# Two layers written out, and each first projection taken by halves of the rows

## The reference, cut to what matters

```python
for l in range(2):                                  # the two layers
    h = h + rmsnorm(mixer(rmsnorm(h, g1[l]) @ w_in[l], ...), g2[l])   # q, k, v of attention, then gated linear attention
    h = h + rmsnorm(swiglu(rmsnorm(h, g3[l])), g4[l])
# the block: the gain is (1 + scale), and a shift is added; both come from c @ w_ada
# then forgetting attention, block attention, and 32 experts of which each row takes 4
```

## Time and profile before

| | |
|---|---|
| median of 3 runs | 1845.13 us (1838.79 to 1845.82) |
| the profiled execution's own time | 1840.45 us |
| its span (first to last instruction) | 1838.5 us, mean granted TensorE clock 0.993 |
| TensorE busy | 1756.8 us, 96% of the span |
| its weight loads | 1038.4 us, 56% |
| VectorE, ScalarE, GpSimd busy | 638.6, 477.6, 123.4 us |

### The profile page before, as it was taken

How to read it: one execution, slowest core, us unless ns; L and a number is a source line. 1 busy time by engine, 2 the same in 40 slices (tenths; PEclk the granted TensorE clock), 3 DMA queues, 4 the chain that set the end, 5 groups by cost and what they waited for, 6 DMA issues and landing times.

```text
span 1838.5 us, 21928 instructions
## 1 busy us (share of the span) xinstructions
PE 1756.8 (96%) x8623; PEld 1038.4 (56%) x8623; DVE 638.6 (35%) x952; ACT 477.6 (26%) x632; POOL 123.4 (7%) x209
## 2 busy tenths in 40 slices
PE   7989999999999999999999999999999999899996
PEld 6776888787678888885534433333334333333332
DVE  3576666546666667242310111111011110011111
ACT  4364443234544333442211111111111111111111
POOL 1031111201111111001000000000000000000000
PEclk9999999999999999999999999999999999999999
DMA  7244776632267776563699999999998999999995
GB/s 272 78 161 150 239 257 230 247 134 96 94 193 252 243 264 225 171 237 113 283 428 428 430 402 405 429 429 428 430 398 346 430 429 430 430 428 430 430 429 248
DMA packets 116361, 559.68 MB, mean 304 GB/s; under 512 B 7460, under 2 KB 52800, under 8 KB 91576
## 3 DMA queue, kind: packets, MB, share of 16 engines
q1 hardware_dynamic: 105904, 526.47, 71.1%
q0 software_dynamic: 9728, 31.94, 5.6%
q10 hardware_dynamic: 648, 0.14, 0.0%
HBM read 557.45 MB, written 1.06 MB: 304 GB/s over the span
## 4 chain that ended last, share of the span: by engine, by line
PE 76%; DMA 12%; issue 5%; DVE 4%; ACT 2%; POOL 0%; ACTq 0%; POOLq 0%; DVEq 0%; SPq 0%
PE PA L1980 13%; DMA ring<-w_down 11%; PE PB L1980 10%; PE PA L2039 5%; PE PB L2039 5%; PE PC L1571 2%; PE PA L1797 2%; PE PD L1797 2%; PE PA L1798 2%; PE PD L1798 2%; PE PD L1804 2%; PE PA L1804 2%; PE PC L2076 2%; PE PD L2076 2%; PE PB L1571 2%
## 5 line engine op out<-in xcount | busy, mean ns | idle before, releaser
L1101 DVE TENSOR_TENSOR ring_rounded<-ring,ring_rounded 128x4096 fp32r<-128x4096 f32 (+2 forms) x53 | 213.1, 4022 | 128.8 <-ACT ring_rounded L776 128.8
L1980 PE MATMUL PA<-ring,HT 128*64 128x512 f32 x944 | 210.0, 595 | 0.2 <-issue 0.2
L1980 PE MATMUL PB<-ring,HT 128*64 128x512 f32 x864 | 194.3, 596 | 6.9 <-DMA ring<-w_gate_up 6.9
L776 ACT ACTIVATE ring_rounded<-ring 128x4096 fp32r<-128x4096 f32 (+2 forms) x53 | 174.9, 3304 | 70.5 <-PE PD L1834 32.8
L2039 PE MATMUL PA<-ring,HT 128*64 128x512 f32 x392 | 135.4, 615 | 8.7 <-DMA ring<-w_down 8.7
L1980 PEld LDWEIGHTS PA<-ring,HT 128*64 128x64 f32 x944 | 66.2, 137 | 131.2 <-issue 131.2
L1980 PEld LDWEIGHTS PB<-ring,HT 128*64 128x64 f32 x864 | 59.5, 137 | 126.5 <-issue 109.3
L2039 PE MATMUL PB<-ring,HT 128*64 128x512 f32 x392 | 127.6, 592 | 0.0
L1480 DVE TENSOR_SCALAR gla<-PA 128x512 f32<-128x512 f32 x17 | 11.8, 692 | 312.2 <-PE PA L1988 312.2
L1495 DVE COPY POSTG<-PB 128x512 f32<-128x512 f32 x17 | 11.8, 692 | 264.7 <-PE PB L2039 264.7
L622 POOL TENSOR_TENSOR stat<-stat,eps 128x1 f32<-128x1 f32 (+2 forms) x28 | 5.4, 191 | 1120.9 <-ACT gla L720 1080.3
(11 more groups left out here) (464 smaller groups left out, 3047.7 us busy)
## 6 DMA issues: line engine op xcount, KB each, us to landing
ring<-w_gate_up SPq DMA_DIRECT2D x106, 2048.0 KB, 19.5
ring<-w_down SPq DMA_DIRECT2D x46, 2048.0 KB, 20.8
ring<-w_in SPq DMA_DIRECT2D x36, 1024.0 KB, 7.4
consts_slot<-w_gate_up SPq DMA_DIRECT2D x14, 2048.0 KB, 16.3
consts_slot<-w_down SPq DMA_DIRECT2D x13, 2048.0 KB, 22.4
prob<-w_ada POOLq DMA_DIRECT2D x96, 256.0 KB, 3.9
ring<-w_gate SPq DMA_DIRECT2D x22, 1024.0 KB, 7.4
ring<-w_up SPq DMA_DIRECT2D x22, 1024.0 KB, 9.8
```

The costliest lines, as they stand in the source:

```text
L776: A_(to, w, ACT.Copy).then_inc(S_["w_coarse"], 1)
L1101: v.tensor_tensor(rest, w, rounding, ALU.subtract).then_inc(S_["w_fine"], 1)
L1980: last = mm((PA, PB)[x][h * SLOTS:(h + 1) * SLOTS, u, :], XT[:, c, x * SLOTS:(x + 1) * SLOTS], expert_slot[slot][:, at:at + BANK], start=c ...
```

## The change

1. The loops over the two layers on four engines become Python loops: each layer's instructions are written out, with fixed semaphore counts.
2. `transposes` and `project_t(l, 0, ...)` give way to `project_first`: transposes of tile 0, three of the four output blocks for tile 0, transposes of tile 1, the fourth block for tile 0, then the four blocks for tile 1. That is 64 matmuls of 128 columns in place of 32 of 256.
3. `fill_ht(l, 0)` becomes `fill_first(l, t)`, four fills of 128x128 on each of the two engines for each tile. For layer 1 and the block, tile 0's fills stand inside the last normalisation of the layer before, ahead of tile 1's squares (ScalarE) and of tile 1's `normed` (VectorE). The rest of the layer start is unchanged: `rows_coarse` still waits for both tiles.
4. ScalarE's copy of the scale and shift (`ada_cols`), VectorE's making of `cols`, and GpSimd's copy of the gains move to that same place. The seven dummy matmuls at the end of a layer become three behind tile 0's transposes.

```diff
@@ TensorE @@
+            def project_first(l):
+                transpose_first(l, 0)
+                pe.wait_ge(*upto("ada_cols", l, 1))
+                if l:
+                    keep_busy(PC[:, 1, :], 3)
+                w = weights(l, 0).rearrange("p (c n) -> p c n", n=BANK)
                 for t in range(T):
+                    pe.wait_ge(*upto("ht_act", l, t + 1))
+                    pe.wait_ge(*upto("ht_dve", l, t + 1))
+                    rows = slice(t * P, (t + 1) * P)
+                    for b in range(4):
+                        if t == 0 and b == 3:
+                            transpose_first(l, 1)
+                        for c in range(KD):
+                            last = mm(PC[:, b // 2, b % 2 * S + t * P:b % 2 * S + (t + 1) * P], w[:, c, b * P:(b + 1) * P],
+                                      HT[:, c, rows], start=c == 0, stop=c == KD - 1)
+                last.then_inc(S_["q_proj"], 1)
...
-            with pe.Fori(0, L) as l:
-                transposes(l, 0)
-                pe.wait_ge(*upto("ada_cols", l, 1))
-                project_t(l, 0, PC, "q_proj")
+            for l in range(L):
+                project_first(l)
...
                 last.then_inc(S_["ada_mod"], 1)
-                keep_busy(PB[:, 1, :], 7)
@@ ScalarE, in norms, between tile 1's two squares @@
+                    if t and n == 1 and l is not L:
+                        act.wait_ge(*upto("ada_mod", l, 2))
+                        A_(modc[:, l:l + 1, :], PC[:, 0:1, 0:2 * KD], ACT.Copy).then_inc(S_["ada_cols"], 1)
+                        fill_first(l + 1, 0)
@@ ScalarE @@
-            with act.Fori(0, L) as l:
-                fill_ht(l, 0)
+            for l in range(L):
+                for t in range(1 if l else 0, T):
+                    fill_first(l, t)
                 rows_coarse(l, 0, INC_LAYER)
                 coarse(l, 0)
@@ VectorE, in residual, behind tile 1's sum, ahead of its normed @@
+                    if t and n == 1 and l is not L:
+                        if l + 1 == L:
+                            steps[0] = 0
+                            block_columns()
+                        fill_first(l + 1, 0)
@@ GpSimd, in norms @@
+                    if t == 0 and n == 1 and l + 1 < L:
+                        layer_gains(l + 1)
```

More of the change, by code:

```diff
@@ L744, in fill_rows, with fill_first, fill_mixed @@
                 last.then_inc(S_["ht_act"], 1)
-            def fill_ht(l, n, halves=range(2)):
-                for half in halves:
[L749 to L753, removed]
+            def fill_first(l, t):
+                act.wait_ge(*upto(("transposed_a", "transposed_b")[t], l, 1))
+                if t == 0 and l is not L:
+                    act.wait_ge(*upto("gains_ready", l, 1))
+                elif t == 0:
+                    act.wait_ge(cols_ready, 1)
+                for c in (0, 1, 4, 5):
+                    rows, src = slice(t * P, (t + 1) * P), (PA, PB)[c // 4][:, 0, c % 2 * S + t * P:c % 2 * S + (t + 1) * P]
+                    if l is not L:
+                        last = A_(HT[:, c, rows], src, ACT.Copy, scale=GC[:, c:c + 1])
+                    else:
+                        last = A_(HT[:, c, rows], src, ACT.Identity, scale=cols[:, 0, c:c + 1], bias=cols[:, 1, c:c + 1])
+                last.then_inc(S_["ht_act"], 1)
+            def fill_mixed(l, halves=range(2)):
+                for half in halves:
+                    act.wait_ge(*upto(("transposed_a", "transposed_b")[half], l, 2))
                     for b in range(2):
@@ L1067, in residual, with fill_first, fill_mixed @@
                         fill_fine(l, t - 1)
+                    if t and n == 1 and l is not L:
+                        assert steps[0] == PER["dve_step"], steps
+                        if l + 1 == L:
+                            steps[0] = 0
+                            block_columns()
+                        fill_first(l + 1, 0)
                     if pre is not None:
                         normed(l, n + 1, pre, t)
-            def fill_ht(l, n, halves=range(2)):
+            def fill_first(l, t):
+                dve.wait_ge(*upto(("transposed_a", "transposed_b")[t], l, 1))
+                if t == 0 and l is not L:
+                    dve.wait_ge(*upto("gains_ready", l, 1))
+                for c in (2, 3, 6, 7):
+                    rows, src = slice(t * P, (t + 1) * P), (PA, PB)[c // 4][:, 1, c % 2 * S + t * P:c % 2 * S + (t + 1) * P]
+                    if l is not L:
+                        last = v.tensor_scalar(HT[:, c, rows], src, GC[:, c:c + 1], None, ALU.mult)
+                    else:
+                        last = v.tensor_scalar(HT[:, c, rows], src, cols[:, 0, c:c + 1], cols[:, 1, c:c + 1], ALU.mult, ALU.add)
+                last.then_inc(S_["ht_dve"], 1)
+            def fill_mixed(l, halves=range(2)):
                 for half in halves:
-                    dve.wait_ge(*upto(("transposed_a", "transposed_b")[half], l, n + 1))
-                    if half == 0 and l is not L:
-                        dve.wait_ge(*upto("gains_ready", l, 1))
+                    dve.wait_ge(*upto(("transposed_a", "transposed_b")[half], l, 2))
                     for b in range(2):
@@ L1207, in _ @@
             dve.wait_ge(filled, 2)
-            with dve.Fori(0, L) as l:
+            for l in range(L):
                 steps[0] = 0
-                fill_ht(l, 0)
+                for t in range(1 if l else 0, T):
+                    fill_first(l, t)
                 rows_fine(l, 0, INF, INC_LAYER)
@@ L1292, in _ @@
                 residual(l, 1, POST_FFN, PRE_MIX)
[L1293 to L1311, removed]
+            fill_first(L, 1)
             rows_fine(L, 0, INF, INC_BLOCK)
```

75 lines of the change are left out of this document (38 added, 37 removed).

## The result

The changed kernel took 1853.59 us, median of 20 runs (1847.10 to 1857.09), against 1845.03 us for the kernel before (20 runs, 1838.79 to 1850.67). The ratio is 1.0048, 95% interval 1.0036 to 1.0060. The forecast was 1842 us and "the same"; the time lies above its range. The sign came out as in rival 2.

The account below looks back on a forecast made before the run. TensorE, busy 96% of the span, was taken as the bound. Terms -3.4 (B) + 3.0 (A) - 0.2 (C) - 0.5 (register arithmetic) gave -1.1 us; between 1839.35 (profiled execution) and 1844.0 (median): 1842 us, range 1834 to 1849.

Parts of the forecast that it names:

- rival 2: Chance 0.10: the clock falls to half in the three new TensorE waits; three falls +10.2 us, 1849.6 us.
- rival 4: Chance 0.01: weight loads don't overlap matmuls, so first-projection passes take 0.22 us each; about +38 us, 1878 us.
- the loop's turn: Before layer 1's transposes: TensorE's 2.9 us of issue disappears when the loop is written out.
- rival 3: Chance 0.12: table loads stay at the starts of layers 0 and 1; total +1.5 us, 1841.95 us.
- A: Kernel start, layer 0's first projection: conversions come later, `v_proj` at 34.1 and not 31.05; loses 3.0 us.
- B: Layer 0 to layer 1: gains 3.4 us, with 2.6 us standing as a new wait for conversions.
- rival 1: Chance 0.13: overlap kept whole, conversions don't bind at the three starts; -7.8 us, 1832.7 us.
- C: Layer 1 to block: biases land 4.1 us later, at 754.9, TensorE waits until 755.0; gains 0.2 us, not 1.65.
- queued transfers slip: Worse end of the range at layer 1 to block: a gain of -0.5 us instead of 0.2.
- register arithmetic: Computed wait counts in the layer loops become constants: 0.5 us saved, from a range of 0 to 1.0.

Follow-up runs that it names:

- e4: Changed kernel with dummy products put into the three new TensorE waits (before `v_proj` in both layers and before `flip(0)`); 1848.61 us, ratio to before 1.0033.
- e9: Kernel before, with the block's distance biases copied only after ScalarE's take of `k_proj`'s result; 1857.52 us, ratio to before 1.0078.
- e8: Changed kernel with weights' conversion and biases' copy moved earlier, layer 0's first projection over whole rows, seven dummies in place of three; 1842.17 us, ratio 0.9985.
- e1: Kernel before with the four layer loops written out and nothing else changed; 1840.70 us, ratio to before 0.9989.
- e10: Kernel before with loops written out and distance biases copied before the forget gate, all first projections over whole rows; 1841.26 us, ratio 0.9981.
- e2: Changed kernel with ScalarE's copy of the distance biases moved before the forget gate's steps; 1843.40 us, ratio to before 1.0000.
- e5: Changed kernel with the first weight chunk's conversion moved ahead of tile 1's part, in both layers and the block; 1838.80 us, ratio to before 0.9972.
- e6: Changed kernel with both the first weight chunk's conversion ahead of tile 1 and the distance biases copied before the forget gate; 1838.32 us, ratio 0.9959.

## Why the prediction was wrong

**Right.** The passes of 128 columns (0.115 measured, 0.112 forecast), so rival 4 is out. The table loads and the loop's turn go, so rival 3 is out. At A the conversions bind, with a wait of 2.35 us and `v_proj` 2.4 us late (2.6 and 3.0 forecast). At B they bind too (2.35, forecast 2.6), so rival 1 is out. B's own gain: TensorE comes to layer 0's one-column products 4.2 late (359.36 against 355.19; the 2.4 of A and what the fall at 35.0 cost) and to layer 1's `v_proj` 2.0 late, so B gave 2.2. The fall at 362.7 took up to 1.7 more; without it B is -3.8 at most, forecast -3.4.

**Wrong, 1: rival 2's rejection.** It was turned down because "B's 2.9 and 1.85 idle passed at 1.00", and had 0.10. That was one execution, which lay low in its kernel's spread with a clock of 0.993 where 85 runs average 0.990. What it showed of a place once was no evidence that the place is safe. The mechanism was there, at about half its price: 5.4 us more lack, against 10.2 for three falls, and B's wait brought none. That the time came out near this rival's 1849.6 is in part luck, since the rest of the loss came from C's term. e4 shows it by taking the falls from the waits, e9 by making one in the kernel before. The rival too had a gap: it looked for falls only behind the new waits. At B and C the clock also fell in the stretch where one-column products are now followed by transposes and three dummies, with seven dummies no longer behind them. e8 doesn't show that the dummies would hold it, and e1 and e10, which keep all seven, had falls at both places as well. What makes it fall in one run and not in the next stays open.

**Wrong, 2: the term of C** ("the biases land 4.1 later too", "waits until 755.0"). They landed at 763.5, 8.6 us later than the forecast 754.9. Carried in from A and B were 2.1 (the one-column products start at 708.58, and at 706.48 before). The place itself then made the conversions 6.8 late (8.9 less 2.1) and not 4.1: 2.7 more. Half clock accounts for that: the one-column products took 1.1 us longer, the eight transposes 0.9 (from 713.18 to 714.92, where a pace of 0.43 for four gives 0.87), the dummies 1.2 (2.56 between starts, forecast 1.3). That is 3.2 in all; the forecast had TensorE waiting for the fills there, which hides some of it. The transfer took 11.8 us and not 8.0: 3.8. TensorE came 3.3 us later than forecast, at 756.9, so the wait was 1.4 + 8.6 - 3.3 = 6.7. The forecast moved the landing by the shift of its issue and kept its length. e2, which issues the same transfer 9.4 us earlier, gets 8.3. What differed is what moved beside it. While the transfer was under way SyncE's queue moved 2.1 MB of weights in the changed kernel and in e4 (11.2 us), 0.64 MB in e5 (8.9), 0.26 in e1 (8.3), 0.02 in the kernel before (8.0) and none in the other eight profiles (7.9 to 8.3, and 8.7 in e6). So it fell together with two weight loads, and the DMA engines' share was 1.00 in 757 to 762. No run moved the loads alone, but in thirteen executions the transfer passed 9 us only in these two. The forecast had allowed 0.5 for "queued transfers slip".

**Too small: the loops.** Written out they gave 4.7 us of rest, not 2.9 at B and 0.5 by register arithmetic. The sum for A compared the halves with the looped kernel's 31.05. Whole rows written out reach `v_proj` at 28.46 (e1), so at A the halves themselves cost 5.0 us, and not 3.0.

**The sum and the range.** Median less 1.1 stood on three runs of before; 85 give the same median, so the level was right and the range missed by its terms alone. Its ends don't follow from its own figures. The lower, by 1839 less 7.8, is 1831 and not 1834. The upper took +4 where rival 2 had priced +9.1; on a level of 1845 that is 1854, and the measured 1853.59 lies there.

## What to carry to other kernels

A wait on the engine that bounds the kernel costs its length and, where the clock then falls, more: here 8 us of delay cost about 13. When work is split in two so that the first half can start early, look at what still stands behind both halves (here the conversion of a weight chunk that needed neither) and move that ahead; that one move turned 0.5% slower into 0.3% faster, of which the loops alone give about 0.1%, not told apart from nothing. Where both halves are ready together anyway, as at the kernel start, leave the stage whole: that gave the fastest kernel, 0.5% under the one before. And when a chain is shifted, price each transfer in it anew by what else is moving at its new time.

## What the runs showed of the hardware

- The spread between executions goes mostly with the clock: 0.984 to 0.993 in 85 runs of one kernel, 0.8 us of span for each us of lack. One profile is one draw of it: e1 and e10 are the same code up to the block, and at the end of layer 0 the clock was at half for 3.4 us in e1 and for 6.8 in e10.
- Away from the span's end, the falls in these profiles lasted 3.4, 6.8 or (e9) 10.2 us, always at half. At the start the full clock came at different points: the same first projection of 64 passes took 14.60 us in e1 and 14.05 in e10. The Trainium skill (TensorE: Matmul & The Clock Gate, Part 1: The HAM clock gate) says that the same kernel gets its full clock after more or fewer products from run to run; these two agree, and the same seems to hold for the falls.
- A transfer of 1 MB on GpSimd's queue landed after 7.9 to 8.9 us where SyncE's queue moved at most 0.64 MB meanwhile (eleven profiles), and after 11.8 in the changed kernel and 11.2 in e4, where it moved 2.1 MB.
- The looped layer's first copy on ScalarE had a table load of 1.28 us before it, at 13.57 and again at 366.46. With the loops written out (e1) neither is there.
